# A two-layer decoder trunk on one core: the second and third norm multiply by the inverse root after the products instead of before

## The reference, cut to what matters

```python
def rmsnorm(x, w):
    return x * lax.rsqrt(jnp.mean(x * x, axis=-1, keepdims=True) + EPS) * w

# layer A: gated DeltaNet beside attention into 256 memory tokens, then a dense SwiGLU
u = rmsnorm(x, norm1)                                   # first norm of the rows
h = x + concat([dn, xa]) @ w_out                        # a_out
h = h + (silu(a) * b) @ ffn_wo                          # a, b = split(rmsnorm(h, norm2) @ ffn_wi), FF = 2816
# layer B: multi-scale pooling beside the same attention, then 2 of 8 experts
up, cq = split(rmsnorm(h, norm1_b) @ w_in)              # b_in: 1024 pooling columns, 512 query columns
h = h + concat([pool(up), xattn(cq)]) @ w_out           # b_out
h = h + moe_swiglu(rmsnorm(h, norm2_b), ...)            # most of the time
```

## Time and profile before

| | us |
|---|---|
| three runs: median, lowest, highest | 1693.0, 1691.19, 1697.15 |
| the profiled execution's own time | 1696.71 |
| its span | 1695.1 |
| busy: PE, DVE, ACT, POOL | 1638.6, 1287.6, 1064.9, 59.5 |
| second norm, last product of `a_out` to first of `wi` | 372.9 to 382.0 |
| third norm, last product of `wo` to first of `b_in` | 577.8 to 586.6 |

### The profile page before, as it was taken

The page is one execution under the profiler, slowest core; times in us unless marked ns, Lnnn a source line. Parts: engine busy times, 40 slices in busy tenths (PEclk is TensorE's granted clock), DMA queues, the critical chain, the costliest instruction groups (busy, mean ns, idle before and its releaser), DMA issues.

```text
span 1695.1 us, 25075 instructions
## 1 busy us (share of the span) xinstructions
PE 1638.6 (97%) x9866; PEld 1420.5 (84%) x9866; DVE 1287.6 (76%) x1160; ACT 1064.9 (63%) x1043; POOL 59.5 (4%) x80
## 2 busy tenths in 40 slices
PE   6999989889999899999999999999999999999997
PEld 6999988889999899888788788788788788788885
DVE  5557868655554565798888888888888888888988
ACT  5556434434443453677777777777777777877775
POOL 0000040000000000110000000000000000000020
PEclk9999989999999999999999999999999999999999
DMA  5664267263554663799999999999999999999993
GB/s 207 252 244 174 101 229 263 82 217 125 176 181 160 252 237 143 287 420 362 372 393 350 385 364 353 399 368 357 389 365 358 388 363 360 384 369 354 385 370 147
DMA packets 74106, 495.24 MB, mean 292 GB/s; under 512 B 8456, under 2 KB 8712, under 8 KB 20656
## 3 DMA queue, kind: packets, MB, share of 16 engines
q1 hardware_dynamic: 65392, 460.71, 71.2%
q0 software_dynamic: 8640, 33.49, 5.4%
HBM read 465.92 MB, written 28.25 MB: 292 GB/s over the span
## 4 chain that ended last, share of the span: by engine, by line
PE 89%; DVE 6%; ACT 4%; issue 1%; DMA 1%; ACTq 0%; SPq 0%; DVEq 0%
PE PP L1696 77%; PE PP L2238 1%; ACT whi L927 1%; PE PP L1987 1%; PE PP L1997 1%; DVE dlo L369 1%; ACT dhi L363 1%; DVE wlo L1486 1%; PE PP L1690 1%; PE PP L1975 1%; ACT L927 0%; PE PP L1777 0%; PE PP L1769 0%; PE PP L1755 0%; DMA ring<-in_wi 0%
## 5 line engine op out<-in xcount | busy, mean ns | idle before, releaser
L1486 DVE TENSOR_TENSOR wlo<-raw,whi 128x2048 fp32r<-128x2048 f32 x336 | 768.1, 2291 | 128.5 <-ACT whi L927 127.9
L927 ACT ACTIVATE whi<-raw 128x2048 fp32r<-128x2048 f32 x336 | 643.8, 1919 | 226.5 <-PE PP L1696 224.6
L1696 PE MATMUL PP<-whi,xsh 128*128 128x512 f32 x896 | 358.2, 400 | 1.8 <-DVE wlo L1486 1.0
L1696 PE MATMUL PP<-whi,xsl 128*128 128x512 f32 x896 | 353.9, 395 | 0.0
L1696 PE MATMUL PP<-wlo,xsh 128*128 128x512 f32 x896 | 353.8, 395 | 0.0
L369 DVE TENSOR_TENSOR dlo<-ring,dhi 128x2048 fp32r<-128x2048 f32 (+2 forms) x86 | 177.8, 2068 | 147.3 <-ACT dhi L363 147.1
L1696 PE MATMUL PP<-uh,dhi 128*128 128x264 f32 x736 | 217.3, 295 | 9.4 <-DVE ul L1037 8.4
L1696 PE MATMUL PP<-ul,dhi 128*128 128x264 f32 x736 | 212.7, 289 | 0.0
L1696 PE MATMUL PP<-uh,dlo 128*128 128x264 f32 x736 | 212.4, 289 | 0.0
L1696 PEld LDWEIGHTS PP<-whi,xsh 128*128 128x128 f32 x896 | 168.6, 188 | 44.1 <-DVE wlo L1486 5.1
L1696 PEld LDWEIGHTS PP<-whi,xsl 128*128 128x128 f32 x896 | 168.6, 188 | 40.1
(11 more groups left out here) (458 smaller groups left out, 1934.7 us busy)
## 6 DMA issues: line engine op xcount, KB each, us to landing
raw<-in_w_e SPq DMA_DIRECT2D x336, 1024.0 KB, 6.0
ring<-in_wi SPq DMA_DIRECT2D x22, 1024.0 KB, 4.8
ring<-in_a_in SPq DMA_DIRECT2D x18, 1024.0 KB, 4.9
slot_rows<-ring POOLq DMA_DIRECT2D x25, 512.0 KB, 16.2
ring<-in_wo SPq DMA_DIRECT2D x16, 704.0 KB, 4.0
ring<-in_mkv SPq DMA_DIRECT2D x8, 1024.0 KB, 4.9
ring<-in_a_out SPq DMA_DIRECT2D x8, 768.0 KB, 4.1
ring<-in_b_in SPq DMA_DIRECT2D x6, 1024.0 KB, 4.8
```

Source lines behind the costliest of these rows:

```text
L927: a.activation(whi[c % XSET][:, :], raw_of(c), ACT.Copy).then_inc(s("w_hi"), 1)
L1486: v.tensor_tensor(wlo[c % XSET][:, :], raw_of(c), whi[c % XSET][:, :].bitcast(F32), ALU.subtract)\
L1696: mm = pe.matmul(out, lhs[l], rhs[r], start=first and i == 0, stop=last and i == 2)
```

## The change

The norm's weight is applied to `h` at once, without the inverse root: as each tile of `h` is ready, ACT copies `h * weight` to `uh` (the weight is the copy's scale), and DVE gives `ul = h * weight - uh`. The products then run on these. The inverse root, which is one number for each of the 264 rows, multiplies what comes out of PSUM: on DVE both banks of a `wi` turn (into `gate_in` and `up_in` in SBUF, which Silu and the product then read) and every `b_in` tile, whose eviction moves from ACT to DVE. DVE adds up the eight tiles of squares as they come, and one product with ones is left, behind the first gate tile and the first `b_in` tile. `wo` uses the banks from 4 on and starts its first tiles before all turns of `wi` are done; the hidden rows' low half of a turn is made one turn later. The split of one chunk (the one behind the last residual tile) comes after the norm's work on that tile instead of before it.

```diff
@@ ScalarE
+                for t in range(KD):
+                    tiles_ = last(t)
+                    for n in tiles_[:-1] if t == KD - 1 else tiles_:
+                        next_high(n)
+                    a.wait_ge(s("h_new"), (i - 2) * KD + t + 1)
+                    a.activation(uh[i - 1][:, t * T:(t + 1) * T], h[:, t, :], ACT.Copy, scale=gains[:, b + t:b + t + 1])\
+                        .then_inc(s("m_hi"), 1)
+                    a.activation(sq[:, t * T:(t + 1) * T], h[:, t, :], ACT.Square).then_inc(s("norm_sq"), 1)
+                next_high(tiles_[-1])
                 a.wait_ge(s("norm_ss"), i + 1)
...
-            high(uh[1], u, T, range(KD), lambda k: a.wait_ge(s("norm_u"), 3 * KD + k + 1))
             for f in range(FT):
-                a.wait_ge(s("wi_mm"), f + 1)
+                a.wait_ge(s("norm_u"), 3 * KD + f + 2)
                 if f >= 2:
                     a.wait_ge(s("wi_prod"), f - 1)
-                a.activation(sil[f % 2], bank(2 * (f % 4))[:, 0:T], ACT.Silu).then_inc(s("wi_sil"), 1)
+                a.activation(sil[f % 2], gate_in[f % 2], ACT.Silu).then_inc(s("wi_sil"), 1)
                 next_high(AT["wi", f])
@@ VectorE
                     v.tensor_tensor(h[:, t, :], h[:, t, :], bank(banks[t])[:, 0:T], ALU.add).then_inc(s("h_new"), 1)
-                    next_low(AT[CHUNKS[name], chunks * (t + 1) - 1])
+                    if t < KD - 1:
+                        next_low(AT[CHUNKS[name], chunks * (t + 1) - 1])
+                    scaled(i, t, g)
+                next_low(AT[CHUNKS[name], chunks * KD - 1])
+
+            def scaled(i, t, g):
+                m_lo[0] += 1
+                v.wait_ge(s("m_hi"), m_lo[0])
+                v.scalar_tensor_tensor(out=ul[i - 1][:, t * T:(t + 1) * T], in0=h[:, t, :], scalar=gains[:, g + t:g + t + 1],
+                                       in1=uh[i - 1][:, t * T:(t + 1) * T].bitcast(F32), op0=ALU.mult, op1=ALU.subtract)\
+                    .then_inc(s("m_lo"), 1)
+                v.wait_ge(s("norm_sq"), i * KD + t + 1)
+                if t:
+                    ins_ = v.tensor_tensor(sq[:, t * T:(t + 1) * T], sq[:, t * T:(t + 1) * T], sq[:, (t - 1) * T:t * T], ALU.add)
...
+            inverse_root(2, rs)
...
+            for f in range(FT):
+                v.wait_ge(s("wi_mm"), f + 1)
...
+                v.tensor_tensor(gate_in[f % 2], bank(2 * (f % 4))[:, 0:T], rs[:, 0:T], ALU.mult).then_inc(s("norm_u"), 1)
+                link(v.tensor_tensor(up_in[f % 2], bank(2 * (f % 4) + 1)[:, 0:T], rs[:, 0:T], ALU.mult))
+                v.wait_ge(s("wi_sil"), f + 1)
...
+                v.tensor_tensor(hidf[f % 2], sil[f % 2], up_in[f % 2], ALU.mult).then_inc(s("wi_prod"), 1)
+                if f:
+                    hidden_low(f - 1)
+                if f < FT - 1:
+                    next_low(AT["wi", f])
+            hidden_low(FT - 1)
+            next_low(AT["wi", FT - 1])
+            residual("wo", 2, [4, 5, 6, 7, 0, 1, 2, 3], 3, GB1)
+            inverse_root(3, rsb)
...
+                if t < XH:
+                    v.tensor_tensor(cq[:, t, :], src[:, 0:T], rsb, ALU.mult).then_inc(s("bin_out"), 1)
+                else:
+                    m = POOL_ORDER[t - XH]
+                    v.tensor_tensor(pin[:, m, PW:PW + SEQ], src[:, 0:SEQ], rsb[:, 0:SEQ], ALU.mult)
+                    v.tensor_tensor(psm_in[:, m, :, PW], src[:, SEQ:T], rsb[:, SEQ:T], ALU.mult).then_inc(s("bin_out"), 1)
@@ TensorE
-            pe.wait_ge(s("h_new"), KD)
-            norm(2, T)
+            def sum_squares(i):
+                pe.wait_ge(s("norm_u"), 3 * KD + 1 + (FT + 1) * (i - 2))
+                pe.matmul(bank(SUM_BANK[i])[:, 0:T], ones[:, :], sq[:, (KD - 1) * T:KD * T], start=True, stop=True)\
+                    .then_inc(s("norm_ss"), 1)
...
                 for g in range(2):
+                    if f == 0:
+                        pe.wait_ge(s("h_new"), KD - 1 + g)
                     mm = tile(bank(2 * (f % 4) + g)[:, 0:T], [x[:, :, g, :] for x in w], 0, (uh[1], ul[1]), T, square,
                               ready=(lambda i: base_f + i + 1) if f == 0 and g == 0 else None)
+                    if f == 0 and g == 0:
+                        sum_squares(2)
                 mm.then_inc(s("wi_mm"), 1)
-            pe.wait_ge(s("wi_prod"), FT)
             for t in range(KD):
+                if t % 2 == 0:
+                    pe.wait_ge(s("wi_prod"), min(FT, FT - 3 + t // 2))
...
-            for t in range(5):
+            b_tile(0)
+            sum_squares(3)
+            for t in range(1, 5):
                 b_tile(t)
```

More of the change, by code:

```diff
@@ L215, in build @@
         assert 2640 + 4096 <= SCN
+        gate_in = [cut(gen, SC + 3168 + 264 * i, 264) for i in range(2)]
+        up_in = [cut(gen, SC + 3696 + 264 * i, 264) for i in range(2)]
+        rsb = cut(ring, 21560, 264)
         sqq = [cut(gen, SC + ACTW * i, ACTW) for i in range(8)]
@@ L832, in _, with residual_norm @@
             dense_high(a, AT["a_out", 1])
[L834 to L842, removed]
+            def residual_norm(i, last, b):
+                for t in range(KD):
[7 more added lines that the diff above has]
+                next_high(tiles_[-1])
                 a.wait_ge(s("norm_ss"), i + 1)
[L844 to L847 removed]
+                a.activation(rt[:, 0:T], bank(SUM_BANK[i])[:, 0:T], ACT.Sqrt, bias=epsc[:, 0:1], scale=1.0 / D)\
+                    .then_inc(s("norm_rt"), 1)
+            residual_norm(2, lambda t: [AT["a_out", t]], GA2)
             for f in range(FT):
[L849 removed]
+                a.wait_ge(s("norm_u"), 3 * KD + f + 2)
                 if f >= 2:
                     a.wait_ge(s("wi_prod"), f - 1)
[L852 removed]
+                a.activation(sil[f % 2], gate_in[f % 2], ACT.Silu).then_inc(s("wi_sil"), 1)
                 next_high(AT["wi", f])
@@ L855, in _ @@
                 a.activation(hidh[:, f * T:(f + 1) * T], hidf[f % 2], ACT.Copy).then_inc(s("hid_hi"), 1)
[L856 to L871, removed]
+            residual_norm(3, lambda t: [AT["wo", 2 * t], AT["wo", 2 * t + 1]], GB1)
             cat_hb = cath[1].rearrange("p (k t) -> p k t", t=T)
@@ L1375, in _, with residual @@
             v.wait_ge(s("S_stored"), 16)
-            def residual(name, chunks, banks=range(8)):
+            def residual(name, chunks, banks, i, g):
                 for t in range(KD):
@@ L1382, in residual, with inverse_root, hidden_low @@
                     v.tensor_tensor(h[:, t, :], h[:, t, :], bank(banks[t])[:, 0:T], ALU.add).then_inc(s("h_new"), 1)
-                    next_low(AT[CHUNKS[name], chunks * (t + 1) - 1])
[L1385 to L1393, removed]
+                    if t < KD - 1:
[11 more added lines that the diff above has]
+                    ins_ = v.tensor_tensor(sq[:, t * T:(t + 1) * T], sq[:, t * T:(t + 1) * T], sq[:, (t - 1) * T:t * T], ALU.add)
+                    if t < KD - 1:
+                        link(ins_)
+                    else:
+                        ins_.then_inc(s("norm_u"), 1)
+            def inverse_root(i, dst):
+                v.wait_ge(s("norm_rt"), i + 1)
+                v.reciprocal(dst[:, 0:T], rt[:, 0:T]).then_inc(s("norm_rs"), 1)
+                v.wait_ge(s("norm_rs"), i + 1)
+            residual("aout", 1, [2, 3, 4, 5, 6, 7, 0, 1], 2, GA2)
+            inverse_root(2, rs)
+            def hidden_low(f):
                 v.wait_ge(s("hid_hi"), f + 1)
@@ L2095, in _ @@
                             pe.wait_ge(s("hid_lo"), km + 1)
-                        mm = split_product(bank(t)[:, 0:T], [x[:, kw, :] for x in w],
+                        mm = split_product(bank((4 + t) % 8)[:, 0:T], [x[:, kw, :] for x in w],
                                            [x[:, km * T:(km + 1) * T] for x in (hidh, hidl)], km == 0, km == FT - 1)
                     mm.then_inc(s("wo_mm"), 1)
-            pe.wait_ge(s("h_new"), 2 * KD)
-            norm(3, T)
             base_b = base_f + KD
```

44 lines of the change are left out of this document (26 added, 18 removed).

## The result

Five runs gave a median of 1681.32 us (1677.47 to 1682.94), beside 1693.09 for the kernel before (five runs, 1691.19 to 1697.15). The ratio is 0.9921, interval 0.990 to 0.9942: 13.4 us less by the ratio, 11.8 by the medians, where 20.2 were forecast. The first profiled execution took 1679.96 us (span 1678.4), two later ones 1687.09 and 1679.97.

The account below looks back on a forecast made before the run. Products on TensorE were taken to bound wi, with TensorE idle and its clock falling at the norms. Terms of 10.4 and 9.8 us sum to 20.2: 1693.0 less 20.2 gives 1672.8 us, range 1667 to 1682.

Parts of the forecast that it names:

- Rival 1: At the norms: small idle pieces still drop the clock, 2.7 us kept per norm; gain 15 us, 1678; chance 0.07.
- Rival 2: Layer B's mixer: VectorE bounds it and TensorE waits for evictions; gain 12.7 us, 1680; chance 0.14.
- Rival 4: At the norms: first products wait for something else, such as a chunk 2 to 4 us later; 1677 to 1681; chance 0.05.
- First term: Second norm through wi and wo: wo ends 10.4 us earlier.
- second chunk: Start of wo: its second chunk is ready at about 4.9 us, the first chunk's products last 4.0; 0.5 of 0.9 gained.
- Turn 2: In wi: chunk 2 is late once, so this turn starts at 386.7 after 0.9 us idle.
- rival 3: wi loop becomes a ring of 7.05 us a turn: 1699; chance 0.03 whole, 0.04 for a few tenths a turn.
- Third norm: Ahead of b_in: first tile starts at 578.2 and tile 3 ends at 590.3, 11.0 us ahead of before.
- tile 4: In b_in: needs the third eviction at about 590.0, just in time; waits 1.0 us if the table load drains.
- Second term: Layer B's mixer: 10.8 us ahead at the pooling product, 1.0 longer tail, so it ends 9.8 us ahead.
- chunk 4's late landing: In b_in: load queues behind memory keys, lands near 600, passes 0.3 to 0.5 us to TensorE at attention's transposes.
- VectorE's tail: Mixer's end: VectorE is the path, and two evictions lengthen it from 8.7 by 1.0, to near 9.7 us.

Follow-up runs that it names:

- e3: Changed kernel with the third norm computed as in the kernel before, only the second norm changed; median 1688.1 us, ratio 0.9950 to before.
- e8: Changed kernel with memory keys loaded behind chunk 4, prompt share ahead of pooling sums, samples' low half earlier; median 1677.5 us, ratio 0.9891 to before.
- e5: Changed kernel with three more unread VectorE multiplies in each of the 22 feed-forward turns; median 1687.6 us, ratio 0.9957 to before.
- e2: Changed kernel with VectorE's share of the second 128 rows ahead of the first pooling sums; median 1678.2 us, ratio 0.9891 to before.
- e1: Changed kernel with the memory keys' loads issued behind b_in chunk 4 instead of ahead; median 1677.9 us, ratio 0.9886 to before.
- e6: Kernel before, with nine unread filler products on TensorE behind the ones products of each norm; median 1695.1 us, ratio 0.9997 to before.
- e4: Changed kernel with the second norm computed as in the kernel before, only the third norm changed; median 1691.9 us, ratio 0.9968 to before.
- e9: Changed kernel with unread filler products on TensorE in the mixer's two short waits; median 1679.9 us, ratio 0.9907 to before.

## Why the prediction was right, and where its sizes were off

The median, 1681.3 us, lies at the upper end of the recorded range of 1667 to 1682, and outside the 1669 to 1677 to which the forecast gave 0.67. The upper part of the range was kept for rivals 1, 2 and 4, and none of them came as described. The gain was forecast in the right stages and by the right mechanism, the two waits removed, at 20.2 us where 11.8 (medians) to 13.4 (ratio) came. That the median still lies in the range is in part luck: two of the five runs, 1682.9 each, and the second profiled execution lie above it.

**First term, 10.4 us: right, at the upper end of what came.** Up to `wo`'s end the changed kernel's three profiles gained 9.3, 9.4 and 10.3 us, e3 10.3 and e8 10.5. Two things move it. The first product of `wi` follows the last of `a_out` by 0.4 to 1.6 us, by when the first weight chunk lands: in the first profile ScalarE stood 3.51 us for that load before it could split the chunk. And `wo` takes 64.7 to 65.3 us where 64.4 were forecast: its second chunk keeps TensorE waiting 0.56 us in each of the three (about 0.4 was booked), and in the second profile a later one 0.27 more. Turn 2 waited 0.63 (0.9 forecast), turns stayed at 5.80 with 0.8 us spare, and e5 shows that this spare time is the point from which rival 3 decides. Rival 4's mechanism is there (`wi` does wait for the chunk), at 0.6 us more than forecast in the worst profile, not at 2 to 4.

**Third norm: right within 0.5 us.** The first tile follows 1.0 us behind `wo` (0.7 forecast), the evictions on VectorE take 0.43 or 0.42 + 0.17, tile 4 doesn't wait, and tile 3 ends 10.5 us ahead of before (11.0 forecast): 13.3 us behind the start of the last `wo` product, where it was 23.8. The root follows the start of its table load by 1.30 us, as in the earlier trace rows. By "ScalarE: Activation LUTs" of the Trainium skill (What ACT_TABLE_LOAD costs), which adds 1380 ns of drain, it would have come 1.38 us later; the trace disagrees, as it did before.

**Second term, 9.8 us: too large, by one wait and by the clock.** The term that was mis-sized is the 0.3 to 0.5 us that chunk 4's late landing was to pass on. The chain was named rightly, but it passed on 1.81 to 2.00 us. Chunk 4's load was forecast to be issued at 589.6 and to land near 600 on the old axis. In the first profile it was issued at 576.60 + 3.88 + 9.28 = 589.8, when the 9.28 us really gained by `wo`'s end are put on, and landed at 602.4: the issue as forecast, the landing 2.4 us late. The prediction gives no working for the 0.3 to 0.5, and it leaves no room for the 4 us of pooling sums that the program has between the split and the share. e2 changes only that order, and its mixer comes out at 62.6 us, 9.7 less than before: the term as forecast, in an execution without a fall of the clock. VectorE's tail was right, 9.65 us for 9.7.

**The clock: a term that was not in the sum.** The sum gave the clock nothing in the mixer, although its own tail, 1.0 us longer, meant a longer wait of TensorE there. Rival 1 put a fall at the norms, where there was none. It came at the two small waits of the mixer instead, and cost about 1.6 us each time. In the first profile 9.8 - 4.3 = 5.5 us were missing in the mixer: 3.2 of it are the two falls, 1.5 the wait beyond what I had booked, and 0.8 lie in smaller pieces, such as 0.3 us more ahead of the first `b_in` product. Without any fall (second profile) the mixer gained 7.5 us.

**The total.** The first profile's span is 16.7 us shorter: 3.9 upstream of the change, 13.8 from the stages up to the experts, less 0.9 behind them. The ratio's 13.4 has an interval of 9.8 to 16.9 us (0.9942 to 0.990 of 1693), which holds the 13.8 and not the 20.2. The second profile, 1687.1, shows how an execution goes to the other end: it reached the last `a_out` product 5.4 us later than the first, and lost 3.5 in the gather at a clock that fell there. Rival 2 (TensorE waits for evictions) gave nearly the right time for the wrong reason: TensorE never waited for one.

Still open is what decides in an execution whether a wait of 1.7 us lets the clock fall.

## What to carry to other kernels

When work is moved earlier by 10 us, follow every load behind it again: one that used to come early enough may now be queued behind a bulk transfer, and what its lateness costs depends on what the waiting engine's order puts between it and its reader. Here the late landing alone (e2) and the order alone (e1) cost nothing, and together 1.9 us. What a norm's idle TensorE cost was the wait; the fallen clock behind it was worth only 0.9 to 1.0 us a norm in e6, because another engine fed the first products one by one. And compare stages from a mark upstream of the change: here the same kernel reached the mark up to 5.4 us apart, as much as two of the effects that were sought.

## What the runs showed that I had not expected

The granted clock falls behind waits of 1.66 to 2.0 us in some executions and not in others of the same kernel (behind four of twelve such waits of the mixer without fillers, and behind none of the six places with them). Two more in e5, of 1.66 us in `wi` and 1.57 in `wo`, had none either. In the earlier trace rows a fall came with an idle 4.2 us. So the length of a wait alone does not tell. The gather ahead of the experts, with the same code, took 17.7 to 18.0 us in eleven profiles and 21.2 to 21.4 in three (e4, the changed kernel's second and e9's second). The window there has a clock of 0.73 in the changed kernel's second profile and of 0.90 in its first, while TensorE idles as long in both (3.9 and 3.8 us):

```profile
675.00:697.00 22.00, 18.07 (x99) 16.34 (x97) 15.33 (x34) 11.30 (x18) 0.00 (x0) 0.73 0.75 298
```

```profile
673.40:691.10 17.70, 13.86 (x93) 12.21 (x92) 14.72 (x32) 10.91 (x17) 0.00 (x0) 0.90 0.74 299
```

"TensorE: Matmul & The Clock Gate" of the Trainium skill (What's actually happening) says that the number of slow products at a kernel's start changes from run to run with the gate's phase. These traces show a change from run to run in the middle of a kernel too, worth 3.5 us in the gather; whether the phase decides it, no run here shows.
